# A transformer step on one core: the rotary shuffle of 25 heads, done by small DMAs instead of VectorE

## What is computed

```python
def rmsnorm(x, g):
    xf = x.astype(jnp.float32)
    y = xf * lax.rsqrt(jnp.mean(xf * xf, axis=-1, keepdims=True) + EPS)
    return (y * g.astype(jnp.float32)).astype(x.dtype)

def apply_partial_rope(x, cos, sin):          # first block: 16 of 64 rows of a head
    half = ROPE_DIM // 2
    xr = x[..., :ROPE_DIM].astype(jnp.float32)
    x1, x2 = xr[..., :half], xr[..., half:]
    rot = jnp.concatenate([x1 * cos - x2 * sin, x2 * cos + x1 * sin], axis=-1).astype(x.dtype)
    return jnp.concatenate([rot, x[..., ROPE_DIM:]], axis=-1)
...
q = jnp.concatenate([q[..., :MLA_NOPE], _rope(q[..., MLA_NOPE:], positions)], axis=-1)   # second block: rows 64 to 95
```

## Time and profile before

| | |
|---|---|
| median of 3 runs | 2448.56 us (2443.29 to 2450.21) |
| the profiled execution's own time | 2450.21 us |
| its span (first to last instruction) | 2448.4 us |
| TensorE busy | 2399.8 us, 98% |
| VectorE / ScalarE / GpSimd busy | 1204.4 / 945.8 / 1314.2 us |
| mean granted TensorE clock | 0.994 of full |
| DMA engines, mean share | 29% |

### The profile page before, as it was taken

The page is one execution under the profiler, slowest core; times in us unless marked ns, Lnnn a source line. Parts: engine busy times, 40 slices in busy tenths (PEclk is TensorE's granted clock), DMA queues, the critical chain, the costliest instruction groups (busy, mean ns, idle before and its releaser), DMA issues.

```text
span 2448.4 us, 28879 instructions
## 1 busy us (share of the span) xinstructions
PE 2399.8 (98%) x11108; PEld 1934.8 (79%) x11108; DVE 1204.4 (49%) x1950; ACT 945.8 (39%) x1471; POOL 1314.2 (54%) x1593
## 2 busy tenths in 40 slices
PE   7999999999999999999999999999999999999999
PEld 7777778888888888777787888888887767788887
DVE  4898756423224532359634843333324686266331
ACT  4454433322224223456524432332325654344321
POOL 4764236656556655536345765555554363456554
PEclk9999999999999999999999999999999999999999
DMA  5221113333333333212122333333332221223333
GB/s 175 78 78 52 52 52 97 99 98 95 96 103 108 95 95 102 85 54 71 59 74 83 93 95 103 95 95 95 96 101 69 61 69 52 86 86 95 96 103 95
DMA packets 59608, 213.35 MB, mean 87 GB/s; under 512 B 6608, under 2 KB 6736, under 8 KB 59344
## 3 DMA queue, kind: packets, MB, share of 16 engines
q1 hardware_dynamic: 59472, 211.52, 29.0%
HBM read 209.39 MB, written 2.10 MB: 86 GB/s over the span
## 4 chain that ended last, share of the span: by engine, by line
PE 84%; DVE 12%; issue 2%; ACT 1%; POOL 0%; DMA 0%; SPq 0%; DVEq 0%; ACTq 0%
PE banks L674 83%; DVE t L1548 1%; DVE t L1146 1%; DVE t L1135 1%; DVE t L1127 1%; DVE t L1121 1%; DVE t L1553 1%; DVE t L1407 1%; DVE t L1143 1%; DVE t L1137 1%; DVE t L1245 1%; DVE t L1128 1%; DVE t L1551 1%; ACT t L1595 0%; PE banks L933 0%
## 5 line engine op out<-in xcount | busy, mean ns | idle before, releaser
L674 PE MATMUL banks<-t,t 128*128 128x512 f32 (+4 forms) x10788 | 2368.1, 389 | 32.9 <-POOL t L1872 15.4
L674 PEld LDWEIGHTS banks<-t,t 128*128 128x128 f32 (+1 forms) x10788 | 1898.9, 189 | 478.0 <-issue 66.1
L1872 POOL TENSOR_TENSOR t<-t,t 128x256 fp32r<-128x256 f32 x1548 | 1255.6, 842 | 1108.1 <-ACT t L1595 1108.1
L1595 ACT ACTIVATE t<-t 128x1024 fp32r<-128x1024 f32 x387 | 409.9, 1059 | 1111.2 <-issue 574.4
L1121 DVE TENSOR_TENSOR t<-banks,t 128x512 f32<-128x512 f32 x121 | 83.2, 688 | 179.9 <-PE banks L674 179.3
L1302 DVE TENSOR_TENSOR t<-banks,t 128x512 f32<-128x512 f32 x44 | 30.4, 691 | 184.5 <-PE banks L674 184.3
L1270 DVE SCALAR_TENSOR_TENSOR t<-banks,t 128x512 f32<-128x512 f32 x32 | 22.1, 692 | 155.4 <-PE banks L674 155.4
L1007 DVE SCALAR_TENSOR_TENSOR t<-t,t,t 128x512 fp32r<-128x512 f32 x64 | 51.5, 805 | 61.9 <-ACT t L1604 61.9
L1247 DVE TENSOR_TENSOR t<-t,t 128x512 fp32r<-128x512 f32 x68 | 70.1, 1030 | 2.3
L1276 DVE TENSOR_TENSOR t<-banks,t 128x512 f32<-128x512 f32 x24 | 16.6, 692 | 106.0 <-PE banks L674 106.0
L1297 DVE TENSOR_TENSOR t<-banks,t 128x512 f32<-128x512 f32 x44 | 30.4, 692 | 70.3 <-PE banks L674 69.9
(11 more groups left out here) (176 smaller groups left out, 1279.2 us busy)
## 6 DMA issues: line engine op xcount, KB each, us to landing
t<-in_w SPq DMA_DIRECT2D x387, 512.0 KB, 3.6
t<-in_xT SPq DMA_DIRECT2D x8, 256.0 KB, 6.2
out<-t SPq DMA_DIRECT2D x8, 256.0 KB, 4.6
t<-in_dmask SPq DMA_DIRECT2D x1, 1536.0 KB, 12.2
t<-in_vbias SPq DMA_DIRECT2D x2, 384.0 KB, 4.0
t<-in_c SPq DMA_DIRECT2D x1, 576.0 KB, 8.7
t<-in_pos SPq DMA_DIRECT2D x2, 256.0 KB, 6.5
t<-in_smask SPq DMA_DIRECT2D x1, 256.0 KB, 12.4
```

The source lines that it names most:

```text
L674: return pe.matmul(o, l, r, start=start, stop=stop, skip_group_check=True)
L1595: a.activation(whl[u % 2][:, 0:1024], wraw[u % 3][:, :], ACT.Copy).then_inc(*w_high.next(u))
L1872: p.tensor_tensor(hl[:, 1024:2048][:, c], wraw[u % 3][:, c], as_f32(hl[:, c]), ALU.subtract).then_inc(*w_low.next((u, q)))
```

## The change

The stream shuffle is taken out of `head_in` on VectorE. ScalarE's `head_in` now issues DMAs from its own queue that copy only the rotated rows, exchanged, from the projection into c: four copies of 8 rows by 512 for a head tile of the first block, two of 16 rows for an MLA query head. Each slot has a semaphore of its own for them. `head_rope` waits for it; for the MLA heads its two operations work on the 32 rotated rows alone. In the first block they still cover all 128 rows, where the sine is zero on rows that aren't rotated; for that the three c tiles are filled with zeros once. The chain has one more condition: `head_rope` is issued when the copies have landed by the planned clock.

```diff
+TURN = {1: [(h + 8 - d, h + d, 8) for h in (0, 64) for d in (0, 8)], 2: [(80, 64, 16), (64, 80, 16)]}
...
+        in_turn = [sig(f"turned_rows{i}", 16) for i in range(3)]
...
+            def clear_turned():
+                for i, (a, b_, c) in enumerate(slot_tiles):
+                    v.memset(c, 0.0).then_inc(*v_norm.next(("clear",)))
...
             def head_in(hid):          # vector
-                v.scalar_tensor_tensor(out=b_, in0=H["R"], scalar=H["g"], in1=COS, op0=M_, op1=M_).then_inc(*v_attn.next())
-                v.stream_shuffle(c, H["R"], SHUFFLE[H["table"]]).then_inc(*v_attn.next(("turned", hid)))
+                v.scalar_tensor_tensor(out=b_, in0=H["R"], scalar=H["g"], in1=COS, op0=M_, op1=M_).then_inc(
+                    *v_attn.next(("cosine", hid)))

             def head_rope(hid):        # vector
-                need.wait_ge(*v_attn.at(("turned", hid)))
-                v.scalar_tensor_tensor(out=c, in0=c, scalar=H["turned"], in1=SIN, op0=M_, op1=M_).then_inc(*v_attn.next())
+                turned = in_turn[H["slot"]]
+                need.wait_ge(*turned.at(hid))
+                x = H["roped"]
+                v.scalar_tensor_tensor(out=c[x], in0=c[x], scalar=H["turned"][x], in1=SIN[x], op0=M_, op1=M_).then_inc(
+                    *v_attn.next())
                 need.wait_ge(*v_attn.last())
-                v.tensor_tensor(b_, b_, c, A_).then_inc(*v_attn.next(("roped", hid)))
+                v.tensor_tensor(b_[x], b_[x], c[x], A_).then_inc(*v_attn.next(("roped", hid)))
...
             def head_in(hid):          # scalar
-                reach(need, *H["src"], *([H["before"]] if H["before"] else []))
+                reach(need, *H["src"], *([H["before"]] if H["before"] else []), H["clear"])
+                for to, of, n in H["rows"]:
+                    a.dma_start(c[to:to + n], H["R"][of:of + n]).then_inc(*in_turn[H["slot"]].next(hid))
                 a.activation(a_, H["R"], ACT.Square).then_inc(*a_attn.next(("square", hid)))
...
                 put("head_sum", hid)
+                yield "v", (in_turn[slot], hid)
                 put("head_rope", hid)
...
         put("turns1")
+        put("clear_turned")
```

More of the change, by code:

```diff
@@ L496, in build_program @@
         p_attn = sig("pool_attention")
[L497 removed]
+        SIGS = [in_cols, in_const, in_mask1, in_swm, in_pos, in_vb, in_cm, stored, *in_x, *in_w, *in_turn, t_dense, t_attn, t_stat,
                 v_evac, v_attn, v_norm, a_evac, a_attn, a_norm, w_high, w_low, p_attn]
@@ L2384, in mixer @@
                 put("qup", l, h_, g, sbd)
-                sch.waiting.append(head_chain(("mq", l, h_), R=MQ[h_], g=col(f"qg_{l}"), table=2, turned=TURNED[f"qg_{l}"],
+                sch.waiting.append(head_chain(("mq", l, h_), R=MQ[h_], g=col(f"qg_{l}"), rows=TURN[2], roped=slice(64, 96), clear=turn, turned=TURNED[f"qg_{l}"],
                                               ones=C["ones"], n=96, tiles=mt, src=[(v_evac, ("qup", l, h_))],
```

5 lines of the change are left out of this document (2 added, 3 removed).

## The result

The changed kernel takes 2468.86 us (median of 4 runs, 2467.63 to 2470.91), the kernel before 2446.64 (4 runs, 2443.29 to 2450.21): a ratio of 1.0092 (95% interval 1.0074 to 1.0109), 22 us slower. The forecast was 2460 us, slower, with a range of 2440 to 2476. The direction and the range held. The loss is twice the 11 us forecast: the measured time lies outside the likeliest case of the prediction (2456 to 2467) and about half way from the forecast to the rival "much slower" (2477). The profiled executions, which are compared from here on, have spans of 2470.4 and 2448.4 us, 22.0 apart as well.

The account below looks back on a forecast made before the run. TensorE, busy 98% of the span, bounds the kernel, so VectorE's work counts only where TensorE idles. Terms 2 + 1 + 6 + 1 + 1 = +11 us, added to the median 2448.6, gave 2460 us; range 2440 to 2476.

Parts of the forecast that it names:

- likeliest case of the prediction: Whole kernel: the likeliest case taken by itself, 2456 to 2467 us; the forecast case had chance 0.45.
- much slower: Rival: ScalarE can't issue while it computes, or copies queue behind weight units; +29 us, 2477 us, chance 0.13.
- The shuffles, worth 0: VectorE: 25 shuffles at 0.744 us, 18.6 us less work; the sum of terms counts no gain for it.
- faster: Rival: VectorE's relief decides, with copies issued and landed in under 2 us together; -9, 2440 us, chance 0.19.
- The copies: issue 0.46, landing 2.0: ScalarE's queue: 84 DMAs, each 0.46 us to issue by SyncE's row and 2.0 us to land (bounds 1.0 and 3.6).
- First seven heads, P = 6.6, +2: First block, heads one after the other: period between bank emptyings grows from 6.32 to 6.6 us, +2 in all.
- The other ten heads, +1 (bounds -3 and +10): First block, later heads often in pairs: +3 for later squares, -2 for idle time there, +1 us.
- The slots, +6 (bounds 0 and +8.7): First block: heads hold slots 2.6 us longer, so second dilated items start 8.7 us later with less filler; +6 us.
- The clock, +1 (bounds -2.5 and +3): After the idle time at 300 to 315, TensorE's 5 us at the 1.2 GHz level gets no shorter; +1 us.
- MLA, +1 (bounds -6 and +6): Two MLA layers: four heads each lose a shuffle but gain 0.92 us ahead of each square; +0.5 a layer.
- signs foretold for the profile: 84 issues of about 0.46 us, period near 6.6, square waits 10 us or more, dilated idle 13 to 16, 350-1000 unchanged.
- signs of a wrong prediction: Issues under 0.1 us on ScalarE, VectorE's wait for copies near zero, or a dilated stretch near 42 us.

Follow-up runs that it names:

- no_exchange: Changed kernel with no exchange of rows at all: no shuffle, no copy, no wait; every order as in the changed kernel. 2449.3 us, ratio to before 1.0009.
- sync_issues: Changed kernel with all copies issued from SyncE's queue instead of ScalarE's; the other engines keep their orders. 2520.6 us, ratio to before 1.0293.
- square_first: Changed kernel with ScalarE's square ahead of the copy issues instead of behind them; all other orders unchanged. 2462.0 us, ratio to before 1.0062.
- dummy_issues: VectorE's shuffles in the changed kernel's order, plus as many ScalarE issues copying constants to an unused tile, with no engine using them. 2469.3 us, ratio 1.0086.
- shuffle_new_order: Changed kernel's order on every engine, but VectorE's shuffles are back and no copy is made. 2454.9 us, ratio to before 1.0034.
- late_copies: Order of the kernel before; copies in all heads but the first seven, which keep shuffles; square ahead of issues. 2449.4 us, ratio 1.0006.
- two_of_four: Changed kernel with only two of the four copies per first-block head; MLA heads and orders unchanged. 2455.6 us, ratio to before 1.0039.
- true_costs: Changed kernel replanned, its planner told 0.65 us per copy issue and 1.4 us more until landing. 2473.7 us, ratio to before 1.0108.
- dma_old_order: Copies made as in the changed kernel, but in the order planned for the kernel before. 2465.5 us, ratio to before 1.0072.

## Why the prediction was right, and where its sum was short

The direction was right, and for the first seven heads and the square by the mechanism given; what the order costs came by another way than I had it. The size was not right: every term of the sum was too small, and it took a range 36 us wide to hold the result.

- **The shuffles, worth 0.** Too little: no_exchange shows 5.6 us. The rival "faster" had the right reason for it, with less than its size.
- **The copies: issue 0.46, landing 2.0.** The landing was right: 2.0 in the head above. The issue was not: 0.655 (four in 2.62). I had taken it from SyncE's three loads out of memory; sync_issues shows that the same queue takes 0.66 for this kind of copy. The row was of another kind of transfer.
- **First seven heads, P = 6.6, +2.** This is the step that failed, in two ways. Right was that the issues, the landing, the sine and the sum make the way to the next bank, and that beside it TensorE has a loop of nearly the same length; that is what square_first and dummy_issues show. Wrong was the start. I let the issues begin when the slot comes free (7.6 - P), so that half of every added us would be taken up by the slot. In the trace the slot is free 1.2 us earlier, and the issues begin when the bank is emptied; from there every us is added in full. With the measured sizes my form would have given (7.6 + 1.97 + 2.0 + 2.85) / 2 = 7.2. Counted from the start of the emptying the period is now 0.71 to the first issue (forecast 1.0) + 1.97 for three issues (1.38) + 2.0 + 1.25 for the sine (1.14) + 1.60 for the sum (1.11) = 7.53. Of the 0.9 missing the issues are 0.6, the sum, which now runs beside GpSimd's L1892, 0.5, and the sine 0.1; the earlier start takes 0.3 off. Seven periods of 1.2 are +8; where these heads end, the same emptying comes at 123.92 in the changed kernel and at 115.69 in shuffle_new_order, 8.2 us apart. That is my upper bound, and the one I had given to the rival "much slower" on other grounds (issues that can't run beside computing; they can).
- **The other ten heads, +1 (bounds -3 and +10).** After less shuffle_new_order is 10.5 us at the last dilated item (335.8 and 325.3). With 8 for the first seven heads, 2 to 3 are left for these. That is a remainder and no measurement; late_copies, in the old order and with the square first, gives 3.7 by medians and nothing in its profiled execution. Perhaps somewhat low, well inside the bounds.
- **The slots, +6 (bounds 0 and +8.7).** Right in size, and that was luck: shuffle_new_order is 6.9 us late at that point, 7.7 by the medians of the whole, but 5.1 of the 6.9 are slower matmuls and not the idle time that I reckoned with. The 3.45 of it that fall into the second dilated items (68.30 less 8.7 would be 59.6; it is 63.05) are half of what I put there; the rest arises before them, and the idle time in that stretch rose by 1.5 to 2 us (8.25 to 9.7, and 10.2 in the changed kernel), not to 13 to 16.
- **The clock, +1 (bounds -2.5 and +3).** Too little. Three stretches of 5 us of the changed kernel:

```profile
205.00:210.00 5.00, 1.97 (x6) 0.60 (x6) 4.22 (x8) 4.18 (x7) 2.62 (x3) 0.78 0.06 13
210.00:215.00 5.00, 4.92 (x12) 2.55 (x12) 4.45 (x9) 1.07 (x2) 3.85 (x4) 0.54 0.36 105
...
305.00:310.00 5.00, 4.73 (x25) 3.78 (x23) 2.85 (x5) 2.17 (x4) 2.19 (x3) 0.50 0.35 97
```

  The granted clock falls to 0.54 and 0.50 in the mean of 5 us, at or near the 1.2 GHz level, in two places where it stayed at 1.00 before; TensorE had been idle for 3.0 of 5 us at 205 to 210, in two waits, one for the square (2.06 us in all, begun before 205) and one for VectorE's L1153 (1.69). To the last dilated item the busy time is 6.4 us more for as many matmuls, and over the whole 9.2. Waits for the square were forecast, the slow stretches that follow them were not.
- **MLA, +1 (bounds -6 and +6).** 4.6 us in the profiled executions, of which shuffle_new_order has 1.1. The four kernels that issue ahead of the MLA squares in a new order (the changed kernel, two_of_four, dummy_issues, true_costs) agree on it: 2134.6 to 2135.1 us from the last dilated item to the end, where the kernels in the new order without these issues (shuffle_new_order, no_exchange), or with the square first, take 2128.3 to 2131.1. In the old order the same copies gain 2.8 (medians; 0.7 with the square first). So the sign depends on the order, which I had not seen. A place of the new order, with 2.71 us of TensorE's waiting for a square that stands behind its two issues:

```profile
1153.15 1.44 ACTq L1663 DMA_DIRECT2D t<-t  x2
...
1154.64 0.63 ACT L1664 ACTIVATE t<-t 128x512 f32<-128x512 f32 x1 [0.77 <-issue]
1154.66 1.23 ACTq L1663 DMA_DIRECT2D t<-t  x2
...
1155.32 1.13 PE L677 MATMUL banks<-t,t 128*128 128x512 f32 x2 [2.71 <-ACT t L1664]
```

  Such waits are not the whole of it, though: behind the last dilated item TensorE waits for squares for 4.0 us in all in the changed kernel and for 4.4 in the kernel before. The 4.6 us are 2.8 of busy time and 1.8 of idle time. With the square first the MLA parts of the new order gain 6.2 us (4.6 of it busy time), those of the old order nothing. Which step of the order makes the difference was not singled out, and the cause stays open.

In sum: 8 (first seven) + 2 to 3 (other ten) + 6.9 (slots, with their slow clock) are the 17.4 of the first block, and 4.6 (MLA) make 22.0. As the other ten are a remainder, this sum can't test itself. VectorE's relief is already taken off in it: against no_exchange (2449.3) the copies cost 19.6 us. Most of the signs foretold for the profile came in: 84 issues, though longer ones; VectorE waiting for the copies (14.8 us) with a longer period in the first heads; waits for the square over 10 us; nothing changed at 350 to 1000. Two did not. TensorE's idle time in the second dilated items is 10.2 us, not 13 to 16. And these items were to start 9 to 12 us later; by the mark used here, the end of the fourth item, it is 23.0 us in the changed kernel and 12.1 in shuffle_new_order. Of the signs of a wrong prediction none came: no issues under 0.1 us, no vanishing wait for the copies, no dilated stretch shorter by 8; the stretch, 62.7 us by the marks used here where it was 68.3, shrank by 5.6 where I had 1.8.

What stays open besides is how much of the 9.2 us of clock belongs to the order and how much to the copies: to the last dilated item shuffle_new_order has 5.1 us more busy time than the kernel before, dma_old_order 4.5, and the changed kernel, with both, only 6.4. In the same order as shuffle_new_order, two_of_four has 0.5.

## What to carry to other kernels

Before moving work to DMAs, look at who issues them: four short copies held ScalarE's queue for 2.6 us ahead of the one result that TensorE waited for, to save VectorE 0.74. Put what another engine waits for ahead of such issues: in square_first the square came 1.7 us earlier in the head, and the copies no later. Take an issue's price from a row of the same kind of transfer, not of the same queue. And where a planner orders the program, price the order and the instructions apart: run the new order with the old instructions and the old order with the new ones; here the copies paid in one part of the program only (MLA), only in the old order, and by 2.8 us, or by 0.7, which is not clear of nothing, with the square first.

## What the runs showed of the hardware that was not expected

- The issue of a copy from tile to tile (8 rows of 2 KB, 16 KB) takes 0.655 us on ScalarE's queue and 0.66 on SyncE's, twice the 0.33 of a weight unit of 512 KB on SyncE; 32 KB in 16 rows takes 0.62 to 0.72. Single issues range from 0.51 to 1.23.
- Copies begin no later with the square in front of them (97.33, 0.04 us after the bank is emptied, square_first): the square, itself waiting for the activation L1605, did not hold them. With the issues in front, ScalarE does no work for 1.6 us before the square begins (102.03, the changed kernel).
- The same addition in VectorE (L1147, 128 x 512) takes 0.69 us with nothing beside it (sync_issues) and 1.67 beside GpSimd's L1892 (the changed kernel). A chain that is made later can so become longer by what it then lies beside.
- Idle time of TensorE of 3.0 us of 5 (205 to 210), in a place full of small waits, was followed by 5 us at a mean granted clock of 0.54. What such stretches cost differs from kernel to kernel: 9.2 us of busy time beside 12.8 of idle time in the changed kernel, 1.7 beside 9.8 in dma_old_order.
